# A second pair of projection blocks in the mixer of a hybrid decoder layer, and a new order of its blocks

## The reference, cut to what matters

```python
h = rmsnorm(x, mix_norm)
proj = h @ w_in                                  # (256 x 2048) @ (2048 x 4928)
cq, ckv, kpe, hq, hf, hi, hg = jnp.split(proj, IN_SPLITS, axis=-1)   # 512, 256, 64, 4 x 1024
a = mla_group(cq, ckv, kpe, ...)                 # latent attention, 8 heads
r = hgrn2_group(hq, hf, hi, hg, lb, ...)         # gated linear recurrence, 8 heads
x = x + concatenate([a, r]) @ w_out
```

## Time and profile before

| what | value |
|---|---|
| three timed executions | 1883.32, 1885.39, 1885.45 us, median 1885.39 us |
| the profiled execution, its own time | 1883.42 us |
| its span, first to last instruction | 1881.6 us |
| mixer, first product of slot 0 to last of slot 39 | about 694 to 939 us of the span |
| the one pair of before on PE | about 815.5 to 858.0 us |
| PE busy in the span | 1874.3 us |

### The profile page before, as it was taken

One profiled execution on the slowest core, in us unless ns is written; L12 is line 12 of the kernel. 1 busy time (PEld: TensorE's weight loads), 2 busy tenths in 40 slices (PEclk: granted clock), 3 DMA queues, 4 the chain that ended last, 5 costly groups with the idle time before them and its releaser, 6 DMA issues.

```text
span 1881.6 us, 23322 instructions
## 1 busy us (share of the span) xinstructions
PE 1874.3 (100%) x8811; PEld 1571.3 (84%) x8811; DVE 1599.2 (85%) x2060; ACT 1094.7 (58%) x1487; POOL 93.5 (5%) x98
## 2 busy tenths in 40 slices
PE   9999999999999999999999999999999999999999
PEld 7888888888889888888888888888888888888987
DVE  6999999989999867786676764789999999999986
ACT  7665555555656547556476655656555555555553
POOL 0000000000000001302250000000000000000000
PEclk9999999999999999999999999999999999999999
DMA  9666555656556665455443654455655566655654
GB/s 338 224 197 200 195 197 195 224 202 201 180 186 213 217 227 155 148 190 191 136 156 112 212 190 135 156 187 195 200 188 194 201 207 216 202 198 183 196 193 172
DMA packets 176689, 362.58 MB, mean 193 GB/s; under 512 B 8512, under 2 KB 19776, under 8 KB 175936
## 3 DMA queue, kind: packets, MB, share of 16 engines
q1 hardware_dynamic: 176144, 360.89, 57.5%
q10 hardware_dynamic: 432, 0.19, 0.0%
HBM read 358.95 MB, written 2.10 MB: 192 GB/s over the span
## 4 chain that ended last, share of the span: by engine, by line
PE 94%; DVE 4%; issue 1%; ACT 0%; DMA 0%; POOL 0%; DVEq 0%; SPq 0%; ACTq 0%
PE acc L2087 18%; PE acc L2089 18%; PE acc L2088 18%; PE acc L2076 8%; PE acc L2078 8%; PE acc L2077 8%; PE small L2087 2%; PE small L2089 2%; PE small L2088 2%; DVE w_lo L1374 2%; PE tr L2035 2%; PE small L2288 1%; PE tr L2089 1%; PE tr L2087 1%; PE tr L2088 1%; PE tr L2103 1%
## 5 line engine op out<-in xcount | busy, mean ns | idle before, releaser
L1374 DVE TENSOR_TENSOR w_lo<-w_raw,w_hi 128x1024 fp32r<-128x1024 f32 (+3 forms) x776 | 757.7, 1030 | 55.5 <-ACT w_hi L764 43.3
L764 ACT ACTIVATE w_hi<-w_raw 128x1024 fp32r<-128x1024 f32 (+4 forms) x562 | 499.5, 924 | 135.9 <-PE acc L2089 104.6
L2087 PE MATMUL acc<-w_hi,hT_hi 128*128 128x512 f32 (+1 forms) x966 | 373.2, 386 | 0.0
L2089 PE MATMUL acc<-w_lo,hT_hi 128*128 128x512 f32 (+1 forms) x966 | 371.3, 384 | 0.0
L2088 PE MATMUL acc<-w_hi,hT_lo 128*128 128x512 f32 (+1 forms) x966 | 371.0, 384 | 0.0
L869 ACT ACTIVATE w_hi<-w_raw 128x1024 fp32r<-128x1024 f32 (+1 forms) x190 | 196.7, 1045 | 123.8 <-DVE w_raw L1362 74.6
L1303 DVE TENSOR_TENSOR w_lo<-w_raw,w_hi 128x1024 fp32r<-128x1024 f32 (+1 forms) x166 | 198.9, 1239 | 31.8 <-ACT w_hi L764 30.4
L2087 PEld LDWEIGHTS acc<-w_hi,hT_hi 128*128 128x128 f32 x966 | 181.4, 188 | 34.4 <-DVE w_lo L1374 0.5
L2089 PEld LDWEIGHTS acc<-w_lo,hT_hi 128*128 128x128 f32 x966 | 181.3, 188 | 34.4
L2088 PEld LDWEIGHTS acc<-w_hi,hT_lo 128*128 128x128 f32 x966 | 181.5, 188 | 33.6
L862 ACT ACTIVATE w_hi<-w_raw 128x512 fp32r<-128x512 f32 (+3 forms) x190 | 154.1, 831 | 91.9 <-PE acc L2089 89.6
(11 more groups left out here) (344 smaller groups left out, 2611.4 us busy)
## 6 DMA issues: line engine op xcount, KB each, us to landing
w_raw<-in_ffn_w_down SPq DMA_DIRECT2D x56, 768.0 KB, 4.6
w_raw<-in_ffn_w_down SPq DMA_DIRECT2D x40, 1024.0 KB, 5.2
w_raw<-in_w_in SPq DMA_DIRECT2D x30, 1024.0 KB, 5.1
w_raw<-in_ffn_w_gate SPq DMA_DIRECT2D x58, 512.0 KB, 3.9
w_raw<-in_ffn_w_gate SPq DMA_DIRECT2D x38, 768.0 KB, 4.3
w_raw<-in_ffn_w_up SPq DMA_DIRECT2D x38, 768.0 KB, 4.6
w_raw<-in_ffn_w_up SPq DMA_DIRECT2D x54, 512.0 KB, 4.7
w_raw<-in_ffn_w_up SPq DMA_DIRECT2D x26, 1024.0 KB, 6.0
```

The costliest lines, as they stand in the source:

```text
L764: nc.scalar.activation(piece(w_hi, c % SPLIT, k0, k1, width), piece(raw, c % RAW, k0, k1, width), ACT.Copy).then_inc(hi_done, 1)
L1374: v.tensor_tensor(piece(w_lo, c % RAW, k0, k1, width), piece(raw, c % RAW, k0, k1, width), piece(w_hi, c % SPLIT, k0, k1, width).bitcast(F ...
L2087: mm(dst, lhs_hi, wh, start=first, stop=False)
L2089: return mm(dst, lhs_hi, wl, start=False, stop=last)
```

## The change

- `MIX` becomes cq, hf0, hq0, ckv, hi0, hg0, hf1, hq1, hi1, hg1. hf0 with hq0 is a pair as well, at slots 4 to 11; hf1 with hq1 is at 24 to 31. Each pair has 12 entries in the ring of slots in place of 8. The first step of a half stands after slots 15 and 33.
- The sums of activations, used by both pairs, are made on DVE in `mixer(2)` (one) and `mixer(3)` (two), in a place of SBUF that is free by then. ACT rounds the first in `mixer(3)`, ahead of the squares of x, and the others in the pair, behind the high parts of the first unit. DVE splits the first behind `combine` of the first unit, the others behind the unit's low parts. The first unit needs only the first sums.
- Work by hand moves: the lower bound's exponential and quotient into the first pair; the angles on DVE to `mixer(16)`, in front of the first level's products; the running sums to slots 13 and 32; the transposes of hq0, cq and ckv on PE to slots 14, 16 and 18, those of hq1 to slot 32. cq is taken into a free part of V.
- The first half's outputs: PE `recurrence_outputs(0)` after slot 32 (was 40), ahead of hq1's transposes; ACT `output_squares(0)` in `mixer(33)`, DVE `recurrence_outputs(0)` in `mixer(34)`. Its fill of `small` is now numbered ahead of the second half's steps.

```diff
-        MIX = ["hf0", "hq0", "cq", "ckv", "hi0", "hf1", "hq1", "hg0", "hi1", "hg1"]
+        MIX = ["cq", "hf0", "hq0", "ckv", "hi0", "hg0", "hf1", "hq1", "hi1", "hg1"]
-        STEP0 = {0: 11, 1: 31}
+        STEP0 = {0: 15, 1: 33}
-        number(slots, "mix", 4 * len(MIX) + 4)
+        number(slots, "mix", 4 * len(MIX) + 8)
-        number(fills, "steps", 2 * STEPS)
-        number(fills, "av", 2)
+        for h in range(2):
+            number(fills, f"steps{h}", STEPS)
+            number(fills, f"av{h}", 1)
```

On ACT:

```diff
+                if m == 3:
+                    sums_rounded(0)
                 if m < 4:
                     entry("x2", m)
...
+                if m == 33:
+                    output_squares(0)
+                for h, m0 in ((0, 15), (1, 34)):
+                    if m == m0:
                         turned(qxT, 0, groups[f"hq{h}"])
...
                 for n in range(len(PAIR.raws)):
                     hi_raw(PAIR.raws[n], NW)
-                    hi_made(PAIR.raws[n] + 1, n, NW, "mix_combined")
+                    hi_made(PAIR.raws[n] + 1, len(PAIR.raws) * h + n, NW, "mix_combined")
                     if n == 0:
-                        mixer(21)
+                        if h == 0:
+                            sums_rounded(1)
+                            sums_rounded(2)
+                        mixer(4 * MB[h] + 1)
+                    if n == 1 and h == 0:
+                        bound_exps()
```

On DVE:

```diff
+            def sums_made(n):
+                if n:
+                    dve.wait_ge(ev("mix_sums_made"), n)
+                done(v.tensor_tensor(mS_flat[:], hT_hi[:, 2 * n:2 * n + 2, :].bitcast(F32), hT_lo[:, 2 * n:2 * n + 2, :].bitcast(F32), ALU.add))
+                done.wait()
+                token_sums(mS_sum[:, n, 0, :], [mS_sum[:, n, i, :] for i in range(1, 4)], mS_flat, "mix_sums_made")
...
+                    combine(c, u, NW, "mix_combined")
+                    if n == 0 and h == 0:
+                        sums_split(0)
+                    lo_parts(c, RAW_PARTS, NW, u, "mix_combined")
+                    if n == 0 and h == 1:
                         step_take(STEPS - 2)
                     lo_parts(c + 1, MADE_PARTS, NW)
...
+                    if n == 0 and h == 0:
+                        sums_split(1)
+                        sums_split(2)
+                    if n == 2 and h == 0:
+                        lower_bound()
...
                 if m == 3:
                     bound_shifted()
+                if m in (2, 3):
+                    for n in ((0,), (1, 2))[m - 2]:
+                        sums_made(n)
+                if m == 16:
                     angles()
...
                 for h in range(2):
-                    if m == 42 + 2 * h:
+                    if m == (34, 44)[h]:
                         recurrence_outputs(h)
```

On PE:

```diff
+                if m == 32:
+                    recurrence_outputs(0)
+                if m in (14, 32):
+                    h = (14, 32).index(m)
+                    pe.wait_ge(ev("queries_scaled"), h + 1)
+                    turn_features(groups[f"hq{h}"], 0, of(nat))
...
+                if m == 42:
+                    recurrence_outputs(1)
...
+                pe.wait_ge(ev("mix_sums_split"), n + 1)
                 if first:
-                    pe.wait_ge(ev("mix_sums_split"), len(PAIR.raws))
-                    free(blocks["mix"] + MB)
+                    free(B)
                     pe.wait_ge(lo_done, 2 * c + 2)
-                    product(acc[:, PG, 0, :], *A12, c, 2, NW, True, False)
+                    product(acc[:, G_, 0, :], *A12, c, 2, NW, True, False)
                     pe.wait_ge(lo_done, 2 * c + 4)
```

More of the change, by code:

```diff
@@ L416, in layer, with paired, step_fill @@
         M = slots["mix"]
[L417 to L422, removed]
-        def mix_slot(m):
-            return M + m if m < 4 * MB else M + m + 4
+        MB = [MIX.index(f"hf{h}") for h in range(2)]
+        def mix_slot(m):
+            return M + m + 4 * sum(m >= 4 * MB[h] + 8 for h in range(2))
+        PAIRS = [Duo(0, True, 0, 0, NW, "upupup", [0, 2, 4], [(6, 4), (10, 3), (13, 3)]) for _ in range(2)]
+        for h, d in enumerate(PAIRS):
+            d.place(M + 4 * MB[h] + 4 * h)
+            for r in d.raws:
+                fetches[r], fetches[r + 1] = 2, 0
+        PG = [(blocks["mix"] + MB[h]) % 2 for h in range(2)]
+        def paired(m):
+            return any(4 * MB[h] <= m < 4 * MB[h] + 8 for h in range(2))
+        def step_fill(k):
+            h, l = divmod(k, STEPS)
+            return fills[f"steps{h}"] + l
         def landed(c):
@@ L599, in _, with load_pair @@
             load_duos(1)
-            def load_pair():
-                sides = [slice(starts[n], starts[n] + NW) for n in ("hf1", "hq1")]
+            def load_pair(h):
+                PAIR = PAIRS[h]
+                sides = [slice(starts[n], starts[n] + NW) for n in (f"hf{h}", f"hq{h}")]
                 for n in range(len(PAIR.raws)):
@@ L1044, in mixer @@
                         act.wait_ge(acc_taken[(blocks["mix"] + b) % 2], (blocks["mix"] + b) // 2 + 1)
-                        src = gate if n == "cq" else ckv_nat[:, :, 0:KR * P]
+                        src = V[:, :, 0:NW] if n == "cq" else ckv_nat[:, :, 0:KR * P]
                         if n == "ckv":
@@ L1136, in _ @@
             for m in range(40):
-                if m == 4 * MB:
-                    pair()
-                if 4 * MB <= m < 4 * MB + 8:
+                if m % 4 == 0 and m // 4 in MB:
+                    pair(MB.index(m // 4))
+                if paired(m):
                     continue
@@ L2293, in mixer @@
                     entry("x2", m)
[L2294 to L2303 removed]
+                if m == 32:
[4 more added lines that the diff above has]
+                    turn_features(groups[f"hq{h}"], 0, of(nat))
+                if m == 16:
+                    stands(blocks["mix"] + MIX.index("cq"))
+                    turn_features(groups["cq"], 0, of(V), QR)
+                if m == 18:
+                    stands(blocks["mix"] + MIX.index("ckv"))
+                    turn_features(groups["ckv"], 0, of(ckv_nat), KR)
                 for h in range(2):
@@ L2376, in pair_plain, with pair @@
                         ins.then_inc(slot_used, 1)
-            def pair():
-                for n in range(len(PAIR.raws)):
-                    pair_unit(n)
-                    pair_plain(0, n)
-                pair_plain(1, 0)
-                pe.wait_ge(ev("forgets_scaled"), 1)
-                turn_features(groups["hf1"], 0, of(gate))
-                pair_plain(1, 1)
-                pair_plain(1, 2)
+            def pair(h):
+                for n in range(len(PAIRS[h].raws)):
+                    pair_unit(h, n)
+                    pair_plain(h, 0, n)
+                pair_plain(h, 1, 0)
+                pe.wait_ge(ev("forgets_scaled"), h + 1)
+                turn_features(groups[f"hf{h}"], 0, of(gate))
+                pair_plain(h, 1, 1)
+                pair_plain(h, 1, 2)
             for m in range(40):
-                if m == 4 * MB:
-                    pair()
-                if 4 * MB <= m < 4 * MB + 8:
+                if m % 4 == 0 and m // 4 in MB:
+                    pair(MB.index(m // 4))
+                if paired(m):
                     continue
```

178 lines of the change are left out of this document (72 added, 106 removed).

## The result

The changed kernel takes 1895.9 us (median of 6 executions, 1893.75 to 1900.25), the kernel before 1884.8 us (6 executions, 1883.32 to 1886.29). The ratio is 1.0065 [1.0055, 1.0074]: slower by 11.1 us, where 5.7 were forecast. The direction was right, the size was not, and the time lies outside the range. The profiled execution of the changed kernel took 1898.58 us, 2.7 above its median, so its rows add up to +15.2 against the 1883.42 of before.

A forecast was written before the change was run, and what follows sets the result against it. PE was taken as the bound, busy 1874.3 of 1881.6 us at full clock. Terms -2.0 - 1.2 + 6.0 + 2.9 = +5.7 us on the 1885.4 median gave 1891.1 us; range 1886.5 to 1894.5 us.

The forecast's parts named there:

- Matmuls removed: Second pair: three units each do seven products in place of eight, saving 9 matmuls, 2.0 us.
- The wait in the narrow slots: PE's 1.2 us wait for DVE at the last narrow ckv slot was taken as gone.
- The start of the first pair: Directly behind slot 3, PE waits 4.3 us for DVE, does a product, waits 1.7 more: 6.0 us together.
- The first half's outputs: Behind slot 32: PE waits 2.9 us for DVE to free `small` for the second half's first level.
- The levels of the first half: Angles in mixer(16) done about 1 us before PE asks for the products: 0 us, bounds 0 to 1.5.
- A rule weighed: Skill's rule that idle gaps lower PE's clock; the sum took nothing for it at the 4.3 us gap.
- Rival (3): The clock falls in the 4.3 us gap at the first pair, costing 1.6 us: 1892.7 us, chance 0.20.
- (1): DVE's sums fall into its idle 5.63 us, first wait 0.4 us: 1885.5 us, no change, chance 0.11.
- (2): The second wait doesn't come, as DVE frees `small` before 872.4: 1888.2 us, chance 0.12.
- (4): Neither wait comes and only the gains stand: 1882.2 us, 0.17% less, chance 0.07.
- The range: Whole kernel: 1886.5 to 1894.5 us, holding the forecast, (2) and Rival (3) with 1.5 us of angles; excluding (1) and (4).
- The base of the forecast: Timed median 1885.4 us, 2.0 above the profiled execution of 1883.4, to which 5.7 us were added.

The follow-up runs named there:

- the kernel without waits: The changed kernel with five moves, plus the splits of cq and ckv one and two slots later: no PE wait listed in the mixer; 1880.59 us, ratio 0.9981.
- the first experiment: The changed kernel with all three sums made on DVE in mixer(2), ahead of the split of the last quarter: 1889.24 us, ratio 1.0028.
- the second experiment: The changed kernel with DVE's recurrence_outputs(0) in mixer(33) in place of mixer(34): 1890.45 us, ratio 1.004.
- the last filler kernel: The changed kernel with useless identity products on PE in all three waits, the first 19 ahead of the wait for the split sums: 1890.95 us, ratio 1.0037.
- outputs first: The changed kernel with DVE's recurrence_outputs(0) one slot earlier, in mixer(33): 1890.45 us, ratio 1.004.
- angles earlier: The changed kernel with DVE's angles in mixer(15) in place of mixer(16): 1895.43 us, ratio 1.0062.
- sums early: The changed kernel with DVE's three sums moved to mixer(2), ahead of the split of the last quarter: 1889.24 us, ratio 1.0028.
- first fillers: The changed kernel with 19 useless identity products on PE at the first pair alone, behind the wait for the split sums: 1896.55 us, ratio 1.0062.
- all three: The changed kernel with DVE's sums in mixer(2), outputs in mixer(33) and angles in mixer(15) together: 1884.7 us, ratio 1.0003.
- splits later: The changed kernel with five moves, plus the splits of cq and ckv in mixer(19) and mixer(22), ckv's transposes after slot 20: 1880.59 us, ratio 0.9981.
- squares of cq moved: The five moves with cq and ckv splits later, plus ACT's squares of cq moved from the first pair to mixer(12): 1880.14 us, ratio 0.9981.
- the kernel with five moves: The changed kernel with sums, outputs and angles earlier, ACT's squares of x in mixer(2), and the first pair's A11 product second: 1883.56 us, ratio 0.9996.

## Why the prediction was right and wrong, step by step

- **Matmuls removed**: right. 8802 against 8811, and the kernel without waits gains it.
- **The wait in the narrow slots**: right for the place (no wait at ckv's slots). But another came at the levels, see below.
- **The start of the first pair**: right, to a few tenths. PE's first product began at 721.02 (forecast 720.62), and from PE's end to the product behind the second wait it lost 6.0 us as forecast. The sums on DVE are shown as the cause by the first experiment. DVE's timeline runs as worked out from the earlier trace rows, 0.2 us late from the entry on:

```profile
706.25 1.66 DVE L1338 SCALAR_TENSOR_TENSOR hT_lo<-tr,gains,hT_hi 128x256 fp32r<-128x256 f32 x4 [5.63 <-ACT hT_hi L790]
...
715.87 1.22 DVE L1380 TENSOR_TENSOR w_raw<-w_raw 128x1024 f32<-128x1024 f32 x1
...
718.45 0.68 DVE L1698 TENSOR_TENSOR mS_lo<-mS_sum,mS_hi 128x512 fp32r<-128x512 f32 x1
719.05 4.09 DVE L1392 TENSOR_TENSOR w_lo<-w_raw,w_hi 128x512 fp32r<-128x512 f32 x4
```

- **The first half's outputs**: right. 2.9 us forecast, 2.8 listed and 3.0 from PE's request (904.7) on; the second experiment shows the cause. (The upper bound of 3.2 us has no row behind it.)
- **The levels of the first half**: this step failed. It looked only at when DVE has the level's products, for which it forecast 1 us of reserve. They were indeed ready (788.10 to 789.30 below, PE asks at 790.29). But the level also needs `small` to be free, and DVE takes the step before it out of `small` (791.57, line 1650) behind the angles (from 782.83) and a slot's low parts:

```profile
782.83 0.69 DVE L1591 CAST level_mask<-mask_i 128x1024 uint8<-128x1024 int32 x1
...
788.10 0.69 DVE L1640 TENSOR_TENSOR wave<-wave,qxT 128x512 f32<-128x512 f32 x1
...
789.30 2.36 DVE L1321 TENSOR_TENSOR w_lo<-w_raw,w_hi 128x1024 fp32r<-128x1024 f32 x2
791.57 1.28 DVE L1650 TENSOR_TENSOR AT<-small,ident 128x512 f32<-128x512 f32 x2
```

  PE lost 792.40 - 790.29 = 2.1 us, where I had 0 with at most 1.5. A moved step has to be followed to everything behind it on its engine, and this one had a second waiter. It is the same kind of wait, of `small` for `AT`, as the one of the earlier trace rows that I took as gone for good.
- **A rule weighed**: this step failed, and it was the larger error. "My sum takes nothing for it, because the gap is far shorter than the idleness before a program" compared the gap with the idleness ahead of the program, and no row bore out that a shorter one is harmless. The granted clock fell to 0.50 behind 4.3 us. The Trainium skill (TensorE: Matmul & The Clock Gate, HAM oscillation) says that an idle gap between bursts of matmuls sends the array back to its low clock; the traces here agree, in the three stretches above.
- **Rival (3)** was therefore the right one, with a chance of 0.20, but its price was too small on two counts. It took 1.6 us from the earlier trace rows, and the first stretch cost 2.3. And it held that "the gap of 4.3 us is the only place long enough to ask": the waits of 2.8 and 1.9 us had their own low stretches, 1.7 and 3.3 us. The longest stretch lies behind the shortest wait.
- **Rivals (1), (2), (4)**: none came. (1) was right as a mechanism: with the sums in the idle time the first wait shrinks to 1.2 us, where 0.4 was worked out.
- **The range** took in a low clock once (1.6) and the angles once (1.5), on top of 1891.1 both would have given 1894.2. It could not hold a low clock behind each wait. What the clock costs in a usual execution follows only roughly. From the kernel before at full clock, 1883.4 + 7.9 for the waits gives 1891.3, and the rest to 1895.9 is 4.6 us; the last filler kernel gives 1895.9 - (1890.95 - 0.7) = 5.7, and the profiled execution, a long one, has 7.3. From the median 1884.8 it would be 3.2, but that median holds executions of before at a clock of 0.999.
- **The base of the forecast**: the 2.0 us by which the median of three timed executions lay above the profiled one were added as they stood. Executions of before as long as that median (1885.4) have a clock of 0.999 wherever the record gives it, so the base very likely held a low stretch already, in a kernel that the sum took as free of them.

Still open: why the clock falls behind a wait of 1.6 to 1.9 us in one execution and not in another, and where it falls in the longer executions of before, of which none was profiled. The runs show only how often.

## What to carry to other kernels

Where PE is busy for all but a few microseconds, price the change by where the other engines have idle time, and put added work there: the same three sums on DVE cost 6.7 us more (5.3 beside their own runs) when they stand behind an idle stretch than inside it. Follow a moved step to every waiter behind it on its engine (data and free buffers both), and count a gap on PE as the gap plus a stretch at the low clock. If a gap can't be removed, useless matmuls in it can pay: in the three gaps here they were worth 3.6 us beside their own runs of before.

## What was unexpected of the hardware

- The clock falls behind short waits. Behind the 4.3 us wait it fell in all three traces that have it (the changed kernel, outputs first, angles earlier), behind 2.8 us in all four (changed, sums early, angles earlier, first fillers), behind 1.9 us in three of four (not with the outputs first), behind 1.6 us in two of three (not with the angles earlier). Behind the 2.5 us ahead of the first fillers it fell in both traces. Behind waits of 1.2 to 1.3 us in the mixer it fell in none of four (the kernel before, sums early, all three, the last filler kernel). The cost of a low stretch in the changed kernel was 1.7 to 3.3 us.
- The time follows the clock from one execution to the next: mean granted clock 0.997 in the executions of 1893.75, 1893.98 and 1894.48 us, 0.996 at 1897.32 and 1898.58, 0.995 at 1900.25. The three kernels whose every execution has 1.000 (splits later, squares of cq moved, the last fillers) scatter over only 0.6 to 1.2 us. The profile of the kernel before shows the full clock too, yet its executions scatter over 3.6 us, at 1.000 and 0.999: one profiled execution doesn't show that a kernel is free of low stretches.
- DVE's split of 128x1024 (two operations) took 4.29 us while POOL worked beside it (784 to 788 in the kernel with five moves, POOL busy 3.57 of 4 us), and 2.36 in most places. It is part of the 1.6 us wait there, and stands in the kernel with the splits later too (4.28, POOL busy 3.52), where PE hardly waits. That POOL is the cause is not shown: I saw the two together in these rows and didn't test it by itself.
